# One layer of a hybrid decoder: the first FFN in Strassen slots, S5 tables through DRAM, two weight sums moved to GpSimd

## The reference, cut to what matters

```python
x = x + 0.5 * rmsnorm(swiglu(rmsnorm(x, norm_g[0]), ffn1_w1, ffn1_w3, ffn1_w2), norm_g[1])
mo, st = mixer(rmsnorm(x, norm_g[2]), w_in, ...)      # mLSTM heads | S5 groups | short conv, then w_out
x = x + rmsnorm(mo, norm_g[3])
x = x + 0.5 * rmsnorm(swiglu(rmsnorm(x, norm_g[4]), ffn2_w1, ffn2_w3, ffn2_w2), norm_g[5])
# swiglu(x, w1, w3, w2) = (silu(x @ w1) * (x @ w3)) @ w2
# S5 (in mixer): a diagonal complex recurrence per group; its tables are
# ab = exp(lre*dt) * (cos, sin)(lim*dt), the factors fre, fim, and powers of ab times b and c
```

## Time and profile before

| | us |
|---|---|
| median of 3 runs | 1067.16 |
| lowest and highest | 1066.69, 1067.69 |
| the profiled execution | 1065.74 |
| its span in the profile | 1064.0 |
| PE busy in the span | 1051.5 (99%) |
| DVE, ACT, POOL busy | 633.5 (60%), 415.7 (39%), 95.5 (9%) |
| share of PE in the chain that ended last | 94% |

### The profile page before, as it was taken

The page is one execution under the profiler, slowest core; times in us unless marked ns, Lnnn a source line. Parts: engine busy times, 40 slices in busy tenths (PEclk is TensorE's granted clock), DMA queues, the critical chain, the costliest instruction groups (busy, mean ns, idle before and its releaser), DMA issues.

```text
span 1064.0 us, 21160 instructions
## 1 busy us (share of the span) xinstructions
PE 1051.5 (99%) x8741; PEld 1038.0 (98%) x8741; DVE 633.5 (60%) x1083; ACT 415.7 (39%) x652; POOL 95.5 (9%) x169
## 2 busy tenths in 40 slices
PE   8999999999999999999999999999999999999997
PEld 7999999999999999999999999999999999999997
DVE  6444533433333348797457776978587558557746
ACT  5322214222122244431255643535455235424542
POOL 0000624930000000070000000000000000000000
PEclk9999999999999999999999999999999999999999
DMA  7223222232322241122421116023332232323122
GB/s 253 91 79 95 83 83 96 79 99 79 95 80 83 73 121 65 60 72 92 159 84 61 60 61 228 23 89 132 107 113 88 78 111 91 109 61 106 39 75 85
DMA packets 31508, 99.39 MB, mean 93 GB/s; under 512 B 3780, under 2 KB 6212, under 8 KB 31304
## 3 DMA queue, kind: packets, MB, share of 16 engines
q1 hardware_dynamic: 31432, 98.33, 28.4%
HBM read 93.58 MB, written 4.74 MB: 92 GB/s over the span
## 4 chain that ended last, share of the span: by engine, by line
PE 94%; DMA 2%; DVE 2%; ACT 1%; issue 1%; SPq 0%; DVEq 0%; ACTq 0%
PE ps L2585 50%; PE ps L2751 17%; PE ps L2820 10%; PE ps L2610 4%; PE ps L2679 3%; PE ps L3180 2%; DMA raw<-w 1%; PE ps L2697 1%; PE ps L2617 1%; PE ps L2622 1%; DMA x<-xT 1%; PE ps L3004 0%; DMA raw<-win 0%; PE ps L2963 0%; PE ps L3095 0%
## 5 line engine op out<-in xcount | busy, mean ns | idle before, releaser
L1354 DVE TENSOR_TENSOR wl<-raw,wh 128x1024 fp32r<-128x1024 f32 (+2 forms) x119 | 138.3, 1162 | 238.9 <-ACT wh L710 238.1
L710 ACT CAST wh<-raw 128x1024 fp32r<-128x1024 f32 (+2 forms) x119 | 116.7, 981 | 305.1 <-PE ps L2585 256.4
L2585 PE MATMUL ps<-xh,wh 128*128 128x272 f32 x1072 | 223.4, 290 | 1.0 <-DVE k L2009 1.0
L2585 PE MATMUL ps<-xl,wh 128*128 128x272 f32 x1072 | 221.3, 288 | 0.0
L2585 PE MATMUL ps<-xh,wl 128*128 128x272 f32 x1072 | 221.2, 288 | 0.0
L2585 PEld LDWEIGHTS ps<-xh,wh 128*128 128x128 f32 x1072 | 168.1, 188 | 2.1 <-issue 1.4
L2585 PEld LDWEIGHTS ps<-xl,wh 128*128 128x128 f32 x1072 | 168.5, 189 | 0.0
L2585 PEld LDWEIGHTS ps<-xh,wl 128*128 128x128 f32 x1072 | 167.7, 189 | 0.0
L2820 PE MATMUL ps<-hh,wh 128*128 128x272 f32 x312 | 64.8, 289 | 0.9 <-DVE wl L1354 0.9
L2820 PE MATMUL ps<-hl,wh 128*128 128x272 f32 x312 | 64.6, 288 | 0.0
L2820 PE MATMUL ps<-hh,wl 128*128 128x272 f32 x312 | 64.4, 287 | 0.0
(11 more groups left out here) (574 smaller groups left out, 2262.9 us busy)
## 6 DMA issues: line engine op xcount, KB each, us to landing
raw<-w SPq DMA_DIRECT2D x68, 512.0 KB, 3.6
pair<-w SPq DMA_DIRECT2D x34, 512.0 KB, 4.5
raw<-win SPq DMA_DIRECT2D x25, 512.0 KB, 3.7
raw<-w SPq DMA_DIRECT2D x24, 384.0 KB, 3.1
raw<-w SPq DMA_DIRECT2D x16, 320.0 KB, 2.9
raw<-wout SPq DMA_DIRECT2D x8, 512.0 KB, 3.7
o_yT<-x SPq DMA_DIRECT2D x8, 272.0 KB, 2.2
cs<-cT SPq DMA_DIRECT2D x4, 516.0 KB, 4.6
```

Of the source, the lines that this page charges most:

```text
L710: nc.scalar.copy(wh[par][:, 0:cols], raw[par][:, 0:cols]).then_inc(hi_done, 1)
L1354: V.tensor_tensor(wl[par][:, 0:cols], raw[par][:, 0:cols], wh[par][:, 0:cols].bitcast(F32), ALU.subtract).then_inc(split_done, 1)
L2585: last = mm(ps[:, bank + s, 0:HALF], w[:, kk * P:(kk + 1) * P], a[:, kk, s * HALF:(s + 1) * HALF], start=(kk == 0 and i == 0), stop=(kk == ...
```

## The change

- FFN1 gets `PARTS1 = (8, 5, 5, 4)`: eight plain tiles, then 14 Strassen tiles in three parts, with the code that FFN2 has. There is a fourth part, so each output block gets one more partial sum into `y`. FFN1's last part, ahead of the boundary, has 4 tiles instead of 6. PE's loops over FFN1's units are written out.
- The sums of x for FFN1 are made in part 0: `normed` after the hidden low parts of tiles 5 and 6, the rest between and beside the downs of part 0 (listed in the diff). The hidden values of plain tiles are now scaled by r in a DVE instruction of their own (`scaled`).
- `sum_2` and `sum_4` of all 31 Strassen tiles are made by POOL (`weight_sums`); `load_pair` also waits for `s4_sum`.
- The S5 tables are made wholly within part 0. `s5_scalars(0)` comes after the third unit's low part, (1) and (2) around tile 2; ACT's `angles(0)` after tile 4 and `angles(1)` after tile 5. POOL signals `f_ready` 1 after AR and AI, 2 after `cbd` and the three powers of `vst`, 3 after three powers of `can` and 4 after the fourth. PE waits for `f_ready` 2 before the down of m = 2 (`s5_turns`) and for 3 before that of m = 6 (`s5_taps`). DVE waits for `f_ready` 2 before `form_sums` 2.
- The tables go to DRAM during part 0's downs (1.58 MB before the load of m = 2; 768 KB and 256 KB before that of m = 6; 1 MB and 128 KB at the end), and come back in two transfers of 856 KB behind the loads of m = 5 and m = 7 of FFN1's last part, in 762 KB and 768 KB behind the first MIX loads, and 1 MB, 256 KB and the constants `cst2` behind the fifth and sixth. PE waits for them at `sample_bu` and `gate_turn`, DVE at MIX step 4.
- At the first boundary `post_sums` moves from behind half unit (5, 1) to (5, 2), and `post_spread` from (5, 4) to (6, 1).

The core of the diff:

```diff
-PARTS = (8, 8, 6)
+PARTS1 = (8, 5, 5, 4)
 PARTS2 = (5, 6, 6, 5)
+PARTS = (PARTS1, PARTS2)
+PLAIN = (PARTS1[0], PARTS2[0])
...
# SP: load_pair and the tables
+                    spe.wait_ge(s4_sum, j - 1)
...
+            def tables_out(m):
+                if m == 1:
+                    spe.wait_ge(f_ready, 1)
+                    spe.dma_start(tab_rows[:, 0:NTAB - 256], tabs[:, 0:NTAB - 256]).then_inc(tab_out, 16)
+                if m == 5:
+                    spe.wait_ge(tab_evac, 1)
+                    spe.dma_start(vin_rows[:, 0:1024], vin_new[0][:]).then_inc(vin_out, 16)
+                    spe.dma_start(vin_rows[:, 1024:1536], vin_new[1][:]).then_inc(vin_out, 16)
+                    spe.dma_start(cb_rows, cb_part).then_inc(vin_out, 16)
...
+                        if p == 0 and f == 0:
+                            tables_out(m - 1)
+                            if m == 4:
+                                load_pair(0)
+                        down(m)
+                        if p == len(PARTS1) - 1 and f == 0 and m in (5, 7):
+                            tables_in((m - 5) // 2)
...
# DVE, end of part 0 of FFN1
+                    if t in (5, 6):
+                        for kk in range(4 * (t - 5), 4 * (t - 4)):
+                            normed(0, kk)
+                dve.wait_ge(tab_out, 16)
+                form_sums(0, 0)
+                form_sums(0, 1)
+                lo_form(0, 0, ...)
+                lo_form(0, 1, ...)
+                lo_form(0, 2, ...)
+                down(2)
+                lo_form(0, 3, ...)
+                dve.wait_ge(f_ready, 2)
+                form_sums(0, 2)
+                down(3)
...
# POOL
+            for n in range(SUB - 1):
+                src = [bst[:, r] if n == 0 else vst[:, n - 1, r] for r in range(2)]
+                powers([vst[:, n, r] for r in range(2)], src, False)
+            signal(f_ready)
+            for n in range(SUB):
+                src = [cbd[:, r] if n == 0 else can[:, n - 1, r] for r in range(2)]
+                powers([can[:, n, r] for r in range(2)], src, True)
+                if n >= SUB - 2:
+                    signal(f_ready)
+            def weight_sums(j):
+                w = pairs[j % 2]
+                pool.wait_ge(s13_sum, j + 1)
+                if j:
+                    pool.wait_ge(s4_sum, j)
+                G.tensor_tensor(s2_raw, s1_raw, w[:, A11B], ALU.add).then_inc(s2_sum, 1)
+                if j:
+                    pool.wait_ge(s4_lo, j)
+                pool.wait_ge(s2_sum, j + 1)
+                G.tensor_tensor(s4_raw, s2_raw, w[:, A12B], ALU.add).then_inc(s4_sum, 1)
+            for j in range(STAGE_AT[1]):
+                weight_sums(j)
...
# PE
+                    whole = p < len(PARTS1) - 1
+                    for m in range(2, KD if whole else WHOLE):
+                        if f == 0 and p == 0:
+                            if m == 2:
+                                s5_turns()      # waits for f_ready 2
+                            if m == 6:
+                                s5_taps()       # waits for f_ready 3
+                        enter_down(m)
+                        down(m, range(n))
```

More of the change, by code:

```diff
@@ L34 @@
 FT = D_FF // P
[L35 removed]
+PARTS1 = (8, 5, 5, 4)
 PARTS2 = (5, 6, 6, 5)
[L37 to L38 removed]
+PARTS = (PARTS1, PARTS2)
+PLAIN = (PARTS1[0], PARTS2[0])
+HMAX = max(PARTS1 + PARTS2)
+HSET = max(PARTS1[1:] + PARTS2[1:])
+assert sum(PARTS1) == FT and sum(PARTS2) == FT
+TILES = [(f, p, i, sum(PARTS[f][:p]) + i) for f in range(2) for p in range(1, 4) for i in range(PARTS[f][p])]
+STAGE_AT = (0, FT - PLAIN[0])
+NG = len(TILES)
 KH = KD // 2
@@ new lines, in ffn @@
+            def ffn(f, inputs=None):
+                u0, hb = UP_AT[f], FT * f
+                up_split = lambda u: split(u0 + u, (u0 + u) % 2, (u0 + u) // 2)
+                if f == 0:
+                    inputs()
+                    split_to(2, third_w[0][0], 2)
+                    for kk in range(KD):
+                        input_square(kk)
+                    split_to(3, fourth_w[0], 2)
+                    split(4, 0, 2)
+                input_root(2 * f)
+                input_copy(2 * f, bcs[:])
@@ new lines, in plain_2 @@
+                up_first(1, 0)
+                scaled(1, 0)
+                gated(1, 0)
+                up_first(1, 1)
+                hidden_lo(FT, 0, 0)
+                scaled(1, 1)
+                up_lo(1, 5)
+                gated(1, 1)
+                hidden_lo(FT + 1, 1, 1)
+                up_lo(1, 6)
+                up_first(1, 2)
+                for kk in range(KD // 2):
+                    normed(1, kk)
+                scaled(1, 2)
+                gated(1, 2)
+                up_lo(1, 7)
@@ new lines, in plain_2 @@
+                hidden_lo(FT + 2, 0, 2)
+                for kk in range(KD // 2, KD):
+                    normed(1, kk)
+                dve.wait_ge(out_dma, 16 * EARLY_STORES)
+                form_sums(1, 0)
+                up_lo(1, 8)
+                up_first(1, 3)
+                form_sums(1, 1)
+                lo_form(1, 0, form_lo_t[2][:], form_t3[:], form_hi_t[:, 2], 1.0)
+                scaled(1, 3)
+                up_lo(1, 9)
+                lo_form(1, 1, form_lo_t[0][:], xn[:, 0, 1], form_hi_t[:, 0], 1.0)
@@ new lines, in plain_2 @@
+                gated(1, 3)
+                hidden_lo(FT + 3, 1, 3)
+                form_sums(1, 2)
+                down(0)
+                lo_form(1, 2, form_lo_t[1][:], form_t24[:], form_hi_t[:, 1], -1.0)
+                up_first(1, 4)
+                scaled(1, 4)
+                gated(1, 4)
+                down(1)
+                hidden_lo(FT + 4, 0, 4)
+                form_sums(1, 3)
+                lo_form(1, 3, base_lo_t[:, 0], xn[:, 0, 0], base_hi_t[:, 0], 1.0)
+                down(2)
@@ new lines, in plain_2 @@
+                lo_form(1, 4, base_lo_t[:, 1], xn[:, 1, 0], base_hi_t[:, 1], 1.0)
+                lo_form(1, 5, form_lo_t[3][:], form_t24[:], form_hi_t[:, 3], 1.0)
+                down(3)
+                lo_form(1, 6, base_lo_t[:, 2], xn[:, 1, 1], base_hi_t[:, 2], 1.0)
+                sum_13(first)
+                down(4)
+                down(5)
+                lo_3(first)
+                lo_a22(first)
+                down(6)
+                lo_4(first)
+                down(7)
+                lo_g(first)
@@ L2504, in powers @@
                 link(G.tensor_tensor(out[1], t[0], t[1], sub))
-            for n in range(SUB):
-                src = [cbd[:, r] if n == 0 else ca[:, n - 1, r] for r in range(2)]
-                powers([ca[:, n, r] for r in range(2)], src, True)
             for n in range(SUB - 1):
@@ L2568, in _ @@
             signal(wkb_ready)
+            for j in range(STAGE_AT[1], NG):
+                weight_sums(j)
         @block.tensor
```

938 lines of the change are left out of this document (444 added, 494 removed).

## The result

The changed kernel takes 1076.15 us (median of 4 runs, 1074.71 to 1077.29) beside 1067.43 for the kernel before in the same session: ratio 1.0083, 95% interval 1.0067 to 1.0099. That is 8.7 us slower, where 2.8 us faster was forecast and the range ended at 1073.5. The profiled execution took 1074.71, its span is 1072.9 (1064.0 before).

The account below looks back on a forecast made before the run. PE was taken to bound the kernel, with no slack, so only fewer matmuls save time. -20.8 + 0 + 7.9 + 1.7 + 8.4 = -2.8 us gave 1064.4 us; range 1055 to 1073.5, the forecast's own 1061 to 1068.

Parts of the forecast that it names:

- Fewer matmuls: Fourteen FFN1 tiles go from plain to Strassen: 168 matmuls fewer, 20.8 us less; sign: PE busy falls 20 to 21 us.
- The weight sums: Moving both sums of Strassen tiles from DVE to POOL: worth 0, bounds 0 and +2 us.
- Rival D: Strassen tiles: POOL's sums delay low parts by 0.3 us in each of 31 tiles, +9.3, 1073.8 us; chance 0.05.
- The S5 chain in part 0: PE waits for POOL's `f_ready` 2 before the down of m = 2: +7.9 us, bounds 0 and 13.
- rival C: Part 0: `f_ready` 2 at 132, PE waits 13; boundary 11; 1072 us, 1074 to 1076 with slower clock; chance 0.20.
- Ends of parts with five tiles: FFN1's two more such ends: PE waits for a low part before the third down, +1.7 us (0 to 2.1).
- The boundary: First boundary with four tiles: +5.8 us up to the sums, +2.6 behind; together +8.4, bounds 0.8 and 12.

Follow-up runs that it names:

- e8: The kernel before, with only the second and fourth weight sums of FFN2's 17 Strassen tiles made by GpSimd; 1066.82 us, ratio 1.0010.
- e4: The changed kernel with the second and fourth weight sums of all 31 Strassen tiles back on DVE; 1074.36 us, ratio 1.0060.
- e11: e9 with the second and fourth weight sums of all 31 Strassen tiles back on DVE; 1059.71 us, ratio 0.9942.
- e2: The changed kernel with 54 useless matmuls ahead of PE's wait for the powers of vst in part 0; 1073.15 us, ratio 1.0056.
- e3: The changed kernel with FFN1 in parts of 8, 4, 4 and 6 tiles instead of 8, 5, 5 and 4; 1068.26 us, ratio 1.0005.
- e7: The changed kernel with only the table read-back transfers moved later, as in e6; 1073.26 us, ratio 1.0068.
- e1: The changed kernel with GpSimd making the powers of vst ahead of FRE, FIM and cbd; 1070.97 us, ratio 1.0036.
- e5: The changed kernel with e1 and e3 together, and DVE's low parts of m = 2 and 3 ahead of its GpSimd wait; 1063.60 us, ratio 0.9976.
- e9: e6 with ACT's second half of angles earlier, DVE's low parts of m = 4 and 5 and ACT's rounding of m = 4 moved ahead; 1060.65 us, ratio 0.9943.
- e6: e5 with table read-back transfers moved from FFN1's last part to behind MIX's first loads, the next two later; 1062.19 us, ratio 0.9967.
- e10: e9 with FFN1 in parts of 8, 4, 5 and 5 tiles instead of 8, 4, 4 and 6; 1063.06 us, ratio 0.9973.

## Why the prediction was wrong, point by point

**Fewer matmuls: right.** The windows of FFN2 and of FFN1's Strassen parts run at the pitch that was taken, and 168 instructions are gone. PE's busy time fell by 10.1 us only (1051.5 to 1041.4) and not by the 20 to 21 that were named as a sign: matmuls at half clock count as longer, and so does each one whose modelled end reaches into a wait.

**A reading of the waits.** The prediction calls 1.8 us the largest of PE's waits before. That is the sum of two. The largest single one is this, at the very start of the kernel, and it is there before and after, so the sum does not change:

```profile
PE ps L2916 <- DVE cbd L1892: 2.2, 1, 2.2
```

**The weight sums: 0 fits, within 2 us.** e8 gives 1.0010 with 1.0000 as its lower end, so 0 to 2 us for FFN2's 17 tiles. e4's median leans the same way, by 1.8 us without GpSimd's sums, and e11 shows no difference within 3 us. A price of 1 or 2 us is not excluded. Rival D is out: its mechanism, the collision, is there (1.35 us for 0.69), but DVE's idle time hides it.

**The S5 chain in part 0: the wait was right, its price was not.** The signal was forecast at 127.7, after seven instructions of GpSimd at about 1.7 us, alternating with DVE's, and five free ones. (Against 119.3 that is 8.4 us; the prediction took 7.9 without saying why.) GpSimd's rows:

```profile
113.02 1.55 POOL L2586 TENSOR_TENSOR ptmp<-vst,s5p 128x256 f32<-128x256 f32 x1
114.53 1.66 POOL L2587 TENSOR_TENSOR ptmp<-vst,s5p 128x256 f32<-128x256 f32 x1
...
122.92 1.54 POOL L2586 TENSOR_TENSOR ptmp<-vst,s5p 128x256 f32<-128x256 f32 x1
124.43 0.61 POOL L2587 TENSOR_TENSOR ptmp<-vst,s5p 128x256 f32<-128x256 f32 x1
125.12 0.72 POOL L2589 TENSOR_TENSOR vst<-ptmp 128x256 f32<-128x256 f32 x1
```

Seven instructions between 113.0 and 124.4 take 1.54 to 1.67 us instead of the 0.62 to 0.73 of the earlier trace rows, as forecast; two free ones follow and not five. PE went on at 126.1, a wait of 6.7 where 7.9 was forecast. The step that failed is the clock: the prediction put it aside as an addition to rival C, with 2 to 4 us and no share of the sum, although the sum itself held a wait of 7.9 us. It cost 2.7 here. e2 shows it by itself.

**Ends of parts with five tiles: right.** 0.9 and 0.9 shown, 1.7 forecast.

**The boundary: the place right, the mechanism in part, the size too small by the same term.** The waits up to the squares' sum were 6.3 - 0.8 = 5.5 us (5.8 forecast) and 1.6 behind it (2.6 forecast), 7.1 together for 8.4. What was missed is the clock again, with 3.4 us, behind these two rows of PE:

```profile
400.84 0.36 PE L2715 MATMUL ps<-hh,dw_hi 128*128 128x272 f32 x1 [1.82 <-DVE y L1823]
```
```profile
410.51 0.83 PE L2722 MATMUL ps<-cst,acc 128*128 128x1 f32 x6 [2.65 <-DVE acc L1849]
```

The prediction had thought of the clock only for the wait of 8 us. Here it also fell behind waits of 1.8 and 2.7 us, with shorter ones around them. e3 shows that PE's shorter tail uncovered the waits: with the tail of before the time falls by 8.3 us (8.2 expected). What the waits hang on is not only DVE's and ACT's own work, as the prediction had it. The squares wait for the second load of MIX (rows at e7), which took 6.0 us instead of 4.6, so 1.5 of the 2.7 us are the load's; the prediction had up to 1.3 us for this in its bounds and nothing in its sum. That the waits came out so near the forecast is partly luck, since four other profiles of the same boundary show 2.3 to 3.1 us more of them.

**A term that was not in the sum: the first Strassen tile.** PE waits 1.5 to 1.7 us in it, in all runs that have it. ACT's rounding of the fourth weight sum is released by DVE's last form. That form is written where hidden values lie, so it waits for the last down of part 0, and it stands in DVE's order right behind a low part that begins only 1.3 us after that down:

```profile
171.41 0.62 ACT L894 CAST s_hi<-sums 128x512 fp32r<-128x512 f32 x1 [2.04 <-DVE form_lo L1576]
```

That is read from the rows and was not tried. FFN2 has another order of buffers and no such wait.

**What remains open.** 1.4 us at L3060 (small matmuls of S5 in the mixer) that the profile gives to "issue": 1.2 to 1.5 in e1, e3, e4, e5, e9 and e11, 0.5 in e6, and not among the waits of e2, e7, e8 and e10. And 0.7 us between the second boundary and the end, 0.4 of it in a longer wait for the evacuation `y` in FFN2's last part (0.7 instead of 0.3). No run told their causes apart. Nor did one tell what decides whether the clock falls behind a wait of about 2 us, or how much of the second MIX load's delay is the tables'.

**The numbers together, for the profiled execution.** The sum's terms were -20.8, +7.9, +1.7 and +8.4. Measured were 6.7 for the second, 1.8 for the third, 7.1 for the fourth, and beside them 6.1 for the clock, 1.7 for the first Strassen tile, about 3 for what waits cost beyond their shown idle time, 1.4 at L3060 and 0.7 at the end: -20.8 + 28.5 = +7.7, of 8.9. Rival C, slower with the chain in part 0 and the boundary, had the sign and 1074 to 1076 with the clock, but a chance of 0.20 and a wait of 13 us for its cause; the time came from waits close to the forecast's own and from the clock. The range ended at 1073.5 because it left this addition out.

## What to carry to other kernels

Where an engine bounds a kernel almost alone, each wait that a change gives it should be priced three times: the idle time, the slower clock that can follow it (here always behind waits of 3.8 us and more, and behind about half of those of 1.6 to 2.7 us), and some 0.25 us that the shown idle time leaves out. A change that takes work off the bounding engine has to be looked at where that engine's work was the cover for other chains (here the tail of a part ahead of a boundary), down to the load that ends last in them. A conclusion from one profile should be held against the others of the same code: the wait for the squares was 2.7 us in one and 5.2 to 5.9 in four. And the order within a chain on a side engine is free to choose: what the bounding engine needs goes first (e1), and what the engine beside it owes the bounding one goes ahead of its own waits (e5, e9). With that the same saving of matmuls gave 0.57% (e9) instead of a loss of 0.83%.

## What the runs showed of the hardware that was not expected

- Whether the granted clock falls to half behind a wait of about 2 us differs from execution to execution, for the same wait in the same code. It fell behind waits of 1.6 (e3), 1.8 and 2.7 (the changed kernel), 2.0 (e9), 2.2 (e5) and 2.4 us (e1), and not behind 2.2 (e6) and 2.6 (e10). Of nine waits of 1.9 us at ends of parts with four tiles in e3, e5, e6, e9 and e10 it fell behind three. It fell at or in every wait of 3.8 us or more, and in e2 and e4 also behind waits of 0.5 and 0.8 us two us apart, which passed without a fall in the changed kernel. The slow stretch behind a wait was 3.4 to 7.2 us long, and a matmul took 0.227 us in it instead of 0.125.
- Taking 23.3 us of two-input work off DVE and giving it to GpSimd made DVE's busy time only 5.5 us smaller (e8), as its low parts beside GpSimd's sums took 1.35 us for 0.69. The Trainium skill (SBUF — State Buffer, two separate sides) describes the port pair that VectorE and GpSimd share as an exclusive lock; the doubled durations agree with that.
- GpSimd slows down too. In the changed kernel's part 0, from 113.0 to 124.4, its instructions that take 0.62 us alone took 1.54 to 1.66, and the DVE instructions beside them, which take 1.2 to 1.3 us alone, took 1.6 to 1.8.
